# Ten-layer block on one core: two PSUM banks exchanged, masks after the scores, 28 products of ones ahead of the program

## What is computed

```python
def swiglu_2(h, w_gate, w_up, w_down):
    return (jax.nn.silu(h @ w_gate) * (h @ w_up)) @ w_down

s_s = jnp.einsum('tghd,tgjld->tghjl', qr_t, kg)
mask_s = (pos <= t[:, None, None, None])
p_s = masked_softmax(s_s, mask_s)
o_c = jnp.einsum('tghc,cgv->tghv', p_c, vc_b)
o_s = jnp.einsum('tghjl,tgjlv->tghv', p_s, vg)
return g_t[..., 0:1] * o_c + g_t[..., 1:2] * o_s + g_t[..., 2:3] * o_w
```

## Time and profile before

| what | value |
|---|---|
| median of 3 runs | 1720.39 us (1720.34 to 1723.35) |
| the profiled execution | 1722.22 us |
| its span in the trace | 1720.4 us |
| TensorE matmuls busy | 1694.4 us, 98% of the span, 11902 records |
| TensorE weight loads busy | 1541.1 us, 90% |
| VectorE busy | 1309.6 us, 76% |
| ScalarE busy | 865.0 us, 50% |
| GpSimd busy | 375.7 us, 22% |
| share of TensorE in the chain that ended last | 95% |
| read from HBM | 307.39 MB, 187 GB/s moved on average |

### The profile page before, as it was taken

The page is one execution under the profiler, slowest core; times in us unless marked ns, Lnnn a source line. Parts: engine busy times, 40 slices in busy tenths (PEclk is TensorE's granted clock), DMA queues, the critical chain, the costliest instruction groups (busy, mean ns, idle before and its releaser), DMA issues.

```text
span 1720.4 us, 30077 instructions
## 1 busy us (share of the span) xinstructions
PE 1694.4 (98%) x11902; PEld 1541.1 (90%) x11902; DVE 1309.6 (76%) x1786; ACT 865.0 (50%) x1236; POOL 375.7 (22%) x425
## 2 busy tenths in 40 slices
PE   7999999999999999999999999999999999999999
PEld 7799999898789999899989988888888899988887
DVE  7898889785868988798757867776778765678773
ACT  5875444443655444444444255554555435555542
POOL 0222012535404223600032130002100127330000
PEclk9999999999899999999999999999999999999999
DMA  8246567685106778555646444564455644335560
GB/s 321 104 148 213 197 220 256 230 301 184 58 3 214 250 266 283 175 200 181 226 165 232 140 158 170 175 237 174 147 189 198 223 146 169 125 123 195 192 241 31
DMA packets 50710, 321.00 MB, mean 187 GB/s; under 512 B 7696, under 2 KB 8912, under 8 KB 20144
## 3 DMA queue, kind: packets, MB, share of 16 engines
q1 hardware_dynamic: 36432, 280.61, 45.6%
q0 software_dynamic: 12736, 36.87, 6.6%
q10 hardware_dynamic: 1440, 2.10, 0.3%
HBM read 307.39 MB, written 10.09 MB: 185 GB/s over the span
## 4 chain that ended last, share of the span: by engine, by line
PE 95%; DVE 2%; ACT 2%; issue 1%; DMA 0%; SPq 0%; ACTq 0%; DVEq 0%
PE bank L2364 32%; PE bank L2365 16%; PE bank L2358 12%; PE bank L2359 11%; PE bank L2360 11%; PE bank L2682 1%; PE bank L2574 1%; PE bank L3049 1%; PE bank L3001 1%; PE bank L2756 1%; PE bank L2867 1%; PE bank L2692 1%; PE bank L2643 1%; PE bank L2644 1%; PE bank L2645 1%
## 5 line engine op out<-in xcount | busy, mean ns | idle before, releaser
L1493 DVE TENSOR_TENSOR w_lo<-raw,w_hi 128x1024 fp32r<-128x1024 f32 (+2 forms) x486 | 641.1, 1322 | 203.1 <-ACT w_hi L1040 201.5
L1040 ACT ACTIVATE w_hi<-raw 128x1024 fp32r<-128x1024 f32 (+2 forms) x486 | 538.2, 1114 | 456.7 <-PE bank L2365 246.7
L2358 PE MATMUL bank<-hg,w_hi 128*128 128x256 f32 x1592 | 454.9, 286 | 11.4 <-DVE hg L1498 10.4
L2359 PE MATMUL bank<-hg,w_hi 128*128 128x256 f32 x1592 | 451.5, 284 | 0.0
L2360 PE MATMUL bank<-hg,w_lo 128*128 128x256 f32 x1592 | 451.4, 284 | 0.0
L2364 PE MATMUL bank<-hg,w_hi 128*128 128x512 f32 x1056 | 374.1, 399 | 2.8 <-ACT rms L1049 2.8
L2364 PE MATMUL bank<-hid,w_hi 128*128 128x512 f32 x1056 | 372.9, 397 | 0.0
L2358 PEld LDWEIGHTS bank<-hg,w_hi 128*128 128x128 f32 x1592 | 306.3, 192 | 15.9 <-DVE w_lo L1493 10.8
L2359 PEld LDWEIGHTS bank<-hg,w_hi 128*128 128x128 f32 x1592 | 306.5, 193 | 0.1
L2360 PEld LDWEIGHTS bank<-hg,w_lo 128*128 128x128 f32 x1592 | 306.5, 193 | 0.0
L2365 PE MATMUL bank<-hid,w_lo 128*128 128x256 f32 x1056 | 296.8, 281 | 0.0
(11 more groups left out here) (427 smaller groups left out, 2198.3 us busy)
## 6 DMA issues: line engine op xcount, KB each, us to landing
raw<-in_w SPq DMA_DIRECT2D x189, 1024.0 KB, 4.8
raw<-in_w SPq DMA_DIRECT2D x48, 1408.0 KB, 5.9
raw<-in_w SPq DMA_DIRECT2D x8, 768.0 KB, 5.4
b_rows<-in_s_b_rows POOLq DMA_DIRECT2D x8, 512.0 KB, 7.9
l_rows<-s_powers POOLq DMA_DIRECT2D x64, 64.0 KB, 9.6
s_ca<-cp_s POOLq DMA_DIRECT2D x8, 512.0 KB, 4.5
s_ba<-ba_s POOLq DMA_DIRECT2D x8, 512.0 KB, 7.4
ba_slot<-s_ba POOLq DMA_DIRECT2D x8, 512.0 KB, 5.3
```

What stands on the lines that cost most here:

```text
L1040: act.activation(w_hi[s][:, 0:n], raw[r][:, c * n:(c + 1) * n], ACT.Copy).then_inc(hi_made, 1)
L1493: dve.tensor_tensor(w_lo[s][:, 0:n], raw[r][:, c * n:(c + 1) * n], w_hi[s][:, 0:n].bitcast(F32), ALU.subtract).then_inc(lo_made, 1)
L2358: pe.matmul(psum, w_hi_ap, x_hi_ap, start=first, stop=False, **kw)
L2359: pe.matmul(psum, w_hi_ap, x_lo_ap, start=False, stop=False, **kw)
```

## The change

There are four edits.

1. `wide_banks`: the second half of the up side of odd pairs goes to bank 4 instead of 3, that of even pairs to bank 3 instead of 4. The wait for `rms_made` ahead of the fourth half of pair 0 is gone; a wait for the same value stands ahead of the loop over pairs 1 to 10.
2. `scores`: the products of queries and keys come first, with the first one in a bank clearing it; the masks of all banks come behind them, and a mask covers only the last 128 keys. With b = 1 a mask is then 256 columns instead of 512, with b = 0 it is 512 as before.
3. nsa's `pv`: both products with the compressed values come first, then the others in their old order.
4. Ahead of the first sub-block TensorE waits for `ones_d` (the first memset of GpSimd), forms 22 fp32 products of `ones_d` with itself into bank 7, waits for the first `w_hi`, and forms 6 more. Nothing reads them.

```diff
--- before.py
+++ after.py
@@ -46,6 +46,7 @@
 EPS = 1e-6
 RT = 12
 GT = 3
+BUSY_BEFORE = (22, 6)
 WIDE_FFNS = (3, 4, 5)
 
 CONV_AT = (3, 5, 9, 11)
@@ -292,7 +293,7 @@
 
         def wide_banks(p, side):
 
-            return ((bank[0], bank[1]), (bank[2], bank[3]))[side] if p % 2 else ((bank[5], bank[6]), (bank[7], bank[4]))[side]
+            return ((bank[0], bank[1]), (bank[2], bank[4]))[side] if p % 2 else ((bank[5], bank[6]), (bank[7], bank[3]))[side]
 
         first = 2 * phases[0]["u0"] + 2 * RT
         PLAIN = list(range(first, first + SPLIT)) if phases[0]["kind"] == "rglru" else []
@@ -2470,8 +2471,6 @@
                                 if c == 0:
                                     first_wide_gates()
                                 continue
-                            if p == 0 and side == c == 1:
-                                pe.wait_ge(jrms_made if ph["joint"] else rms_made, 1 if ph["joint"] else ph["norm"] + 1)
                             wide_half(half + 2 * side + c, wide_banks(p, side)[c], it)
 
                 def pair(p, it=0):
@@ -2499,6 +2498,8 @@
                         s5_products(ph, p)
                 else:
                     pair(0)
+                    if ph["wide"]:
+                        pe.wait_ge(rms_made, ph["norm"] + 1)
                     with pe.Fori(0, 5) as it:
                         pair(1, it)
                         pair(2, it)
@@ -2676,10 +2677,12 @@
                     banks = att.score_banks(n, keys)
                     per = 4 // len(banks)
                     for a, x in enumerate(banks):
-                        pe.matmul(x, att.mask_ident, att.mask[:, T - keys:T][:, None, :].broadcast_to([P, per, keys]), start=True, stop=False)
                         for i in range(per):
                             q, k = score(branch, 4 * group + per * a + i, b)
-                            last = pe.matmul(x[:, i, :], q, k[:, 0:keys], start=False, stop=i == per - 1)
+                            pe.matmul(x[:, i, :], q, k[:, 0:keys], start=i == 0, stop=False)
+                    for x in banks:
+                        last = pe.matmul(x[:, :, keys - P:keys], att.mask_ident, att.mask[:, P:T][:, None, :].broadcast_to([P, per, P]),
+                                         start=False, stop=True)
                     last.then_inc(scores_done, 1)
 
                 def turn(n):
@@ -2859,13 +2862,15 @@
                     for i in (0, 2):
                         cols = slice(64 * i, 64 * i + P)
                         pe.matmul(psum[:, cols], vc_s[:, group, i:i + 2, :].rearrange("p i v -> p (i v)"), prob_c[:, b, group, :],
-                                  start=True, stop=False)
+                                  start=i == 0, stop=False)
+                    for i in (0, 2):
+                        cols = slice(64 * i, 64 * i + P)
                         for branch in range(2):
                             v = (v_sel, v_win)[branch]
                             for kt in range(b + 1):
                                 for e in range(2):
                                     last = pe.matmul(psum[64 * e:64 * e + 64, cols], v[:, kt, 64 * group:64 * group + 64],
-                                                     att.prob_t[branch][:, kt, i + e, :], start=False, stop=branch == 1 and kt == b)
+                                                     att.prob_t[branch][:, kt, i + e, :], start=False, stop=i == 2 and branch == 1 and kt == b)
                     return last
 
                 def step_waits(n):
@@ -3121,6 +3126,16 @@
                             last.then_inc(half_used, 1)
                 project(ph, half0 + 16, 1, 8, glu,
                         lambda k: pe.wait_ge(outlo_made, k // 2 + 1), 2)
+
+            def keep_busy(products):
+
+                for _ in range(products):
+                    pe.matmul(bank[7][:, 0:P], ones_d[:, :], ones_d[:, :], start=True, stop=True)
+
+            pe.wait_ge(pool_const, 1)
+            keep_busy(BUSY_BEFORE[0])
+            pe.wait_ge(hi_made, 1)
+            keep_busy(BUSY_BEFORE[1])
             for ph in phases:
                 if ph["kind"] == "ffn":
                     ffn_phase(ph)
```

## The result

The changed kernel took 1707.3 us (median of 6 runs, 1704.58 to 1709.6), the kernel before 1720.1 us beside it (6 runs, 1716.74 to 1723.35). The ratio is 0.9922, with a 95% interval of 0.9910 to 0.9934, so it is faster by 11.4 to 15.5 us. The forecast was 1712.1 with a range from 1707.5 to 1717.

The account below looks back on a forecast made before the run. TensorE was taken as the bound nearly everywhere, with matmuls busy for 98% of the span. Terms 3.3 + 1.7 + 1.2 + 2.1 = 8.3 us off the median 1720.4 gave 1712.1 us, range 1707.5 to 1717.

Parts of the forecast that it names:

- Edit 1, the banks: Three wide blocks: the fourth half no longer waits for the root, 3 x 1.09 = 3.3 us off.
- Edit 2, the masks: Score steps with b = 1 in nsa and moba: masks halved to 256 columns, 1.7 us off in all.
- 0.25 us counted for moba: Masks in moba's 2 score steps with b = 1: half of 0.5 us counted as gain.
- Edit 3, the values: nsa's outputs: grouped records of compressed values take 0.54 instead of 0.74 us a job, 1.2 us off in all.
- Edit 4, the ones: Begin: unread products raise TensorE's clock before 10.44 us, so half 1 starts at 17.04 instead of 19.14, 2.1 us gained.
- The rival of a clock that doesn't rise: Begin: ones do not raise the clock in time; total gain 6.8 down to 4.4 us, about 1714.8; chance 0.22.
- does the lead last?: After the begin: the 2.1 us lead lasts, since weight loads follow TensorE and no long TensorE wait stands on a DMA.
- the third rival: The half-clock stretch behind nsa's long wait goes away: 2 to 5 us more gained, about 1708.5; chance 0.09.
- the second rival: One more half-clock stretch in the attentions costs at most 5.1 us: total gain 3.2 us, 1717.2; chance 0.08.

Follow-up runs that it names:

- the product inside: Changed kernel plus one 256-column fp32 product of ones behind the third pair of passes in the down projections of ffn 1 to 5: 1710.33 us, one execution.
- the fill: Changed kernel plus eight unread fp32 products of ones ahead of nsa's long wait on VectorE's probabilities: 1706.78 us, ratio 0.9917; run again 1706.80 us, 0.9923.

## Why the prediction was right or wrong

**Edit 1, the banks: right about the wait, wrong about what comes behind it, and this is the step that failed.** The stall was worth 4.06 - 2.97 = 1.09 us a block, to the hundredth what rows 5 gave, and no wait on `w_lo` took its place. But the step then took a pair of passes as "0.36 us" (1041.43 to 1041.79) and let it run on unchanged. The term was 3.3 us; it measured 10.0 us in the traces and 10.8 us (8.3 to 13.4) by itself in the runs, since the pace behind the wait changed as well, 2.23 us a block. I had rounded 0.24 + 0.12 and never compared the pace ahead of the wait with that behind it. Both were in the trace: the kernel before ran 0.3467 us a pair in its third half, behind the first pair, and 0.3533 us for 110 us after the stall.

**Edit 2, the masks.** 2.27 to 2.04 us a step, 0.23 us where 0.24 was forecast. By itself it measured 1.5 us (0 to 3.1) against 1.7 us. The wait on VectorE grew as said. The 0.25 us counted for moba did not show (192.57 and 192.58 us).

**Edit 3, the values.** 0.74 to 0.53 us, as forecast, and 0.15 us more for the outputs as a whole, which was not. By itself 1.0 us (-0.5 to 2.4) against 1.2 us, so that run doesn't confirm the term. Together the two edits gave 2.5 or 3.3 us in nsa in the traces (by which low stretch is compared), where 1.4 + 1.2 = 2.6 us were forecast.

**Edit 4, the ones.** The clock rose at 7.1 us, where I said 6.2, still ahead of 10.44; half 1 started at 17.27, where I said 17.04, as the sums of squares began at 13.93 instead of 13.6. The rival of a clock that doesn't rise is out. The Trainium skill (TensorE: Matmul & The Clock Gate, Part 1: The HAM clock gate) says that activity releases the throttle, and here the begin agrees: products that nothing reads did it. The step "does the lead last?" is the weak one. It argued that no long wait of TensorE stood on a DMA; the waits of VectorE on one, 4.8, 0.7 and 0.2 us, were what to look at, and where the lead was lost TensorE had waits on a DMA of its own. The 2.1 us were 1.87 us at the begin and 0.7 us (-1.4 to 2.6) at the end when alone, 0.6 to 1.4 us on top of the other edits.

**The rivals of the low stretch.** The changed kernel's profile shows a shorter stretch, as the third rival had it, and that explains 1.9 to 2.7 of the 17.1 us between the two profiled executions. It does not explain the medians, as far as the traces tell: the same program up to there shows 3.4 to 10.2 us, and that of before 0 to 10.2 us. Had I forecast from this rival, I would have been nearer for a wrong reason. A second low stretch, as the second rival had it, stood in two of the later profiles (388.0 and 449.5 us without the ones, 432.9 and 453.4 us with the product inside), each of 3.4 us; from single profiles it can't be told whether the change makes it more frequent.

**The sum.** 10.0 (traces) + 1.5 + 1.0 + 0.7 (runs) = 13.2 us from the parts, of which the last two are not told apart from nothing, 13.4 us (11.4 to 15.5) from the ratio of the whole. Against the forecast 8.3 us, the pace accounts for more than all of the difference, and the ones gave a little less than said.

## What to carry to other kernels

When a long row of equal matmuls has a stall in it, compare the distance between starts before and behind the stall over a hundred of them, to a nanosecond: in 13 of 15 blocks here a stall of 1.1 us cost another 2.2 us, which no view of waits shows. Where such a stall can't be removed, try a small product behind it, and measure whether it helps, since the same product did nothing at other places. A lead that is won at the begin must be followed through every engine's waits on transfers before it is counted at the end.

## What the hardware did that I had not expected

- Passes of 512 and 256 columns in turn run at one of two paces, 108.16 or 110.24 us for 312 pairs, and keep the one they have for more than 100 us. What stands at the entry to the row can change it, and an fp32 product behind a stall moved it from slow to fast in 3 of 3 blocks.
- The low-clock stretch in nsa was 0, 3.4 or 10.2 us long in executions of one and the same code up to there.
- Ahead of nsa's attention VectorE's waits on the same three transfers were 4.5 us longer in total in the kernel with the ones alone than in the kernel before, and 3.0 us longer in one execution of the changed kernel than in another (9.7 against 6.8 us). In both the lead of about 1.9 us was lost.
- A shorter low stretch gave back less than half of the difference: 6.8 us less of it were worth 2.7 us in one pair of profiles and 1.9 us in another. 3.4 us less, in the changed kernel with the fill, were worth nothing (90.25 and 90.24 us), as TensorE then waited 1.84 instead of 0.26 us for VectorE's probabilities.
